# Second block: beta and decay weights as the stationary side beside the first tile, square sums and decay sums among the tiles, the last norm applied in the scan

## What is computed

```
h = rms_norm(x, norm1_w) * (1.0 + sc1) + sh1            # x: the first block's output, after its own last norm
proj = h @ w_in                                         # 1024 x (1536 + 1536 + 512 + 4 + 4 + 2048)
qa, ka, va, qkv_b, z_b, b_b, a_b, gate_a, gate_b = split(proj)
y_a = moba_attention(qa, ka, va, rel_bias)
qkv_b = silu(causal_depthwise_conv(qkv_b, conv_w))      # 4 taps, 3 * 512 channels
beta = sigmoid(b_b)                                     # 4 heads
g = -exp(a_log) * softplus(a_b + dt_bias)
o_b = gated_delta_rule(q_b, k_b, v_b, beta, g)          # q, k divided by their root of summed squares;
                                                        # cumulative sums of g per chunk of 64; scan over 4 chunks
m = sigmoid(gate_a) * (y_a @ w_up_a) + sigmoid(gate_b) * (rms_norm(o_b) * silu(z_b) @ w_up_b)
x = x + g1 * (m @ w_out)                                # then the mixture of 32 experts
```

## Time and profile before

| | us |
|---|---|
| median of 3 runs (lowest, highest) | 1450.25 (1447.91, 1450.72) |
| the profiled execution | 1449.64 |
| its span, first to last instruction | 1447.9 |
| TensorE busy | 1381.7 (95%) |
| VectorE busy | 767.1 (53%) |
| ScalarE busy | 611.1 (42%) |
| mean granted TensorE clock | 0.973 |

### The profile page before, as it was taken

How to read it: one execution, slowest core, us unless ns; L and a number is a source line. 1 busy time by engine, 2 the same in 40 slices (tenths; PEclk the granted TensorE clock), 3 DMA queues, 4 the chain that set the end, 5 groups by cost and what they waited for, 6 DMA issues and landing times.

```text
span 1447.9 us, 25571 instructions
## 1 busy us (share of the span) xinstructions
PE 1381.7 (95%) x9884; PEld 1189.3 (82%) x9884; DVE 767.1 (53%) x1338; ACT 611.1 (42%) x1016; POOL 10.6 (1%) x23
## 2 busy tenths in 40 slices
PE   6999999999999999989999999999999789999995
PEld 5899989899999798678999989889999755555543
DVE  6456646655554776346666556758546542222213
ACT  4544554533333564345444444656534321121122
POOL 0000020000000000000000000000000000000000
PEclk9999999999999899999999998999999889999999
DMA  9654345655555544367555563332134559999970
GB/s 361 127 180 146 132 161 175 242 173 173 174 174 178 215 143 132 126 239 245 190 181 186 188 235 130 131 114 76 59 102 146 199 205 409 408 405 405 406 306 29
DMA packets 80293, 289.78 MB, mean 200 GB/s; under 512 B 9536, under 2 KB 10560, under 8 KB 80064
## 3 DMA queue, kind: packets, MB, share of 16 engines
q1 hardware_dynamic: 78480, 284.65, 55.1%
q0 software_dynamic: 1712, 3.68, 1.7%
HBM read 285.14 MB, written 3.15 MB: 199 GB/s over the span
## 4 chain that ended last, share of the span: by engine, by line
PE 85%; DVE 8%; ACT 3%; issue 2%; DMA 1%; SPq 0%; DVEq 0%; ACTq 0%
PE bank L746 18%; PE bank L750 17%; PE bank L749 17%; PE bank L1364 12%; PE bank L901 2%; ACT w_hi L1440 1%; DVE ring_low L1872 1%; PE bank L1349 1%; PE bank L1325 1%; PE bank L1326 1%; PE bank L781 1%; PE bank L1350 1%; DMA ring<-weights 1%; PE bank L823 1%; DVE rstd L1904 1%
## 5 line engine op out<-in xcount | busy, mean ns | idle before, releaser
L1872 DVE TENSOR_TENSOR ring_low<-ring,w_hi 128x1024 fp32r<-128x1024 f32 x292 | 356.3, 1224 | 290.2 <-ACT w_hi L1440 287.8
L746 PE MATMUL bank<-hn_hi,w_hi 128*128 128x272 f32 (+1 forms) x1456 | 425.1, 292 | 6.1 <-DVE hn_low L1891 3.9
L750 PE MATMUL bank<-hn_hi,ring_low 128*128 128x272 f32 (+1 forms) x1456 | 418.1, 287 | 0.0
L749 PE MATMUL bank<-hn_low,w_hi 128*128 128x272 f32 (+1 forms) x1456 | 417.6, 287 | 0.0
L1440 ACT ACTIVATE w_hi<-ring 128x1024 fp32r<-128x1024 f32 x292 | 307.1, 1054 | 207.5 <-PE bank L746 174.4
L746 PEld LDWEIGHTS bank<-hn_hi,w_hi 128*128 128x128 f32 x1456 | 277.3, 190 | 12.8 <-DVE hn_low L1891 6.4
L750 PEld LDWEIGHTS bank<-hn_hi,ring_low 128*128 128x128 f32 x1456 | 277.9, 191 | 0.0
L749 PEld LDWEIGHTS bank<-hn_low,w_hi 128*128 128x128 f32 x1456 | 277.5, 191 | 0.2
L746 PE MATMUL bank<-arena_r,w_hi 128*128 128x256 f32 (+1 forms) x848 | 246.7, 291 | 9.1 <-DVE arena_r L2392 3.6
L750 PE MATMUL bank<-arena_r,ring_low 128*128 128x256 f32 (+1 forms) x848 | 243.6, 287 | 0.0
L749 PE MATMUL bank<-arena_r,w_hi 128*128 128x272 f32 (+1 forms) x784 | 225.3, 287 | 0.0
(11 more groups left out here) (386 smaller groups left out, 1620.8 us busy)
## 6 DMA issues: line engine op xcount, KB each, us to landing
ring<-weights SPq DMA_DIRECT2D x436, 512.0 KB, 4.3
tab<-weights SPq DMA_DIRECT2D x32, 512.0 KB, 6.7
w_late<-weights SPq DMA_DIRECT2D x32, 512.0 KB, 8.1
arena<-weights SPq DMA_DIRECT2D x32, 512.0 KB, 5.9
tab<-tables SPq DMA_DIRECT2D x1, 2857.0 KB, 17.6
skew<-arena POOLq DMA_DIRECT2D x1, 2048.0 KB, 46.5
h<-tokens SPq DMA_DIRECT2D x2, 544.0 KB, 4.1
tab<-skew POOLq DMA_DIRECT2D x8, 128.0 KB, 3.5
```

The source lines that it names most:

```text
L746: begun = mm(dst[:, 0:cols], wh, high(k), start=k == 0, stop=False)
L749: mm(dst[:, 0:cols], wh, low(k), start=False, stop=False)
L750: last = mm(dst[:, 0:cols], wl, high(k), start=False, stop=k == K - 1)
L1872: tt_(ring_lo[:, slot, :], ring[:, slot, :], w_hi[:, n % SPLITS, :], ALU.subtract).then_inc(S("w_lo_ready"), 1)
```

## The change

The eight weight columns of beta and decay become the stationary side: in tile 0 each k-step has, beside its own three matmuls, three with `wba` as weights (8 columns) and the 256 tokens moving, into 8 rows of `bank[4]` (`with_decay_inputs`). VectorE copies the 8 rows to `ba_rows`, and behind tile 2 two small products turn them to tokens on partitions. ScalarE reads out tiles 0 to 2 before it makes beta and softplus, VectorE makes the first tap of those tiles before it stores the inputs. The four decay sums are issued behind tile 6, and VectorE stores them before `conv(4)`. The 16 sums of squares are issued one per k-step in qka tiles 6 and 7. The first block's last norm on `h` moves to the scan: its reciprocal ahead of it, two of its 8 products in each chunk.

```
+            def with_decay_inputs(high, low, cols, ready):
...
+                dst, rows = bank[t % BANKS], bank[4][0:8, 0:cols]
...
+                pe.wait_ge(S("wba_split"), 1)
+                for k in range(DT):
+                    ready(k)
+                    cut, ba = slice(k * P, (k + 1) * P), slice(8 * k, 8 * k + 8)
+                    wh, wl = w_hi[:, n % SPLITS, cut], ring_lo[:, unit % SLOTS, cut]
+                    begun = mm(dst[:, 0:cols], wh, high(k), start=k == 0, stop=False)
...
+                    mm(rows, wba_hi[:, ba], high(k), start=k == 0, stop=False)
+                    mm(rows, wba_lo[:, ba], high(k), start=False, stop=False)
+                    last_ba = mm(rows, wba_hi[:, ba], low(k), start=False, stop=k == DT - 1)
+                    mm(dst[:, 0:cols], wh, low(k), start=False, stop=False)
+                    last = mm(dst[:, 0:cols], wl, high(k), start=False, stop=k == DT - 1)
+                last_ba.then_inc(S("ba_done"), 1)
+                last.then_inc(tile_done, 1)
...
-            dense(DT, hb, hb_lo, SEQ, split_ready("n1"))
-            pe.wait_ge(S("wba_split"), 1)
-            for tt in range(2):
-                for k in range(DT):
-                    dst, cut = bank[4][:, 8 * tt:8 * tt + 8], slice(tt * P, (tt + 1) * P)
-                    mm(dst, hn_hi[:, k, cut], wba_hi[:, 8 * k:8 * k + 8], start=k == 0, stop=False)
-                    mm(dst, hn_lo[:, k, cut], wba_hi[:, 8 * k:8 * k + 8], start=False, stop=False)
-                    last = mm(dst, hn_hi[:, k, cut], wba_lo[:, 8 * k:8 * k + 8], start=False, stop=k == DT - 1)
-            last.then_inc(S("ba_done"), 1)
+            with_decay_inputs(hb, hb_lo, SEQ, split_ready("n1"))
             for t in range(1, 12):
                 dense(DT, hb, hb_lo, SEQ)
...
-            for t in range(8):
+            for t in range(6):
                 dense(DT, hb, hb_lo, SEQ)
...
+            for t in range(2):
+                dense(DT, hb, hb_lo, SEQ, lambda k: l2_sum(DT * t + k))
             wide(DT, hb, hb_lo, [(0, P), (P, SEQ)])
...
+            for t in range(3):
+                raw_tile(t)
+            highs(at["qkvb"] + 3)
+            act.wait_ge(S("ba_split"), 2)
             fn(M("beta", 0, 8), M("b", 0, 8), ACT.Sigmoid).then_inc(S("beta_ready"), 1)
...
             lows(at["qkvb"])
             dve.wait_ge(S("ba_done"), 1)
+            nc.vector.tensor_copy(ba_rows, bank[4][0:8, 0:SEQ]).then_inc(S("ba_split"), 1)
+            for t in range(3):
+                conv_first(t)
+            lows(at["qkvb"] + 3)
+            dve.wait_ge(S("ba_done"), 2)
...
+            norm_scale("final", SEQ)
             dve.wait_ge(S("u_stored"), 1)
...
+                for k in range(2 * c, 2 * c + 2):
+                    stt(h[:, k, XC], h[:, k, XC], V("final", k), rstd[:, 0:SEQ], ALU.mult, ALU.mult).then_inc(normed, 1)
```

More of the change, by code:

```diff
@@ L1050, in _ @@
             assert pos[1] == at["qkvb"]
-            dense(DT, hb, hb_lo, SEQ, split_ready("n1"))
-            pe.wait_ge(S("wba_split"), 1)
-            for tt in range(2):
-                for k in range(DT):
-                    dst, cut = bank[4][:, 8 * tt:8 * tt + 8], slice(tt * P, (tt + 1) * P)
-                    mm(dst, hn_hi[:, k, cut], wba_hi[:, 8 * k:8 * k + 8], start=k == 0, stop=False)
-                    mm(dst, hn_lo[:, k, cut], wba_hi[:, 8 * k:8 * k + 8], start=False, stop=False)
-                    last = mm(dst, hn_hi[:, k, cut], wba_lo[:, 8 * k:8 * k + 8], start=False, stop=k == DT - 1)
-            last.then_inc(S("ba_done"), 1)
+            with_decay_inputs(hb, hb_lo, SEQ, split_ready("n1"))
             for t in range(1, 12):
                 dense(DT, hb, hb_lo, SEQ)
[L1064 to L1068, removed]
+                if t == 2:
+                    pe.wait_ge(S("ba_split"), 1)
+                    for tt in range(2):
+                        last = mm(bank[4][:, 8 * tt:8 * tt + 8], ba_rows[:, tt * P:(tt + 1) * P], ident[0:8, 0:8],
+                                  start=True, stop=True)
+                    last.then_inc(S("ba_done"), 1)
+                if t == 6:
+                    pe.wait_ge(S("g_ready"), 1)
+                    g = M("g", 0, 8)
+                    for j, name in enumerate(("upto", "chunk", "half0", "half1")):
+                        last = mm(bank[5][:, 8 * j:8 * j + 8], C(name), g, start=True, stop=True)
+                    last.then_inc(S("g_summed"), 1)
             pe.wait_ge(S("g_stored"), 1)
@@ L1084, in _, with l2_sum @@
             pe.wait_ge(S("beta_rows"), 1)
-            for p in range(2 * NP):
+            def l2_sum(p):
                 last = mm(bank[4][:, p:p + 1], l2sq[:, p * P:(p + 1) * P], ones[:, 0:1], start=True, stop=True)
-            last.then_inc(S("l2_summed"), 1)
+                if p == 2 * NP - 1:
+                    last.then_inc(S("l2_summed"), 1)
+            for t in range(2):
+                dense(DT, hb, hb_lo, SEQ, lambda k: l2_sum(DT * t + k))
             wide(DT, hb, hb_lo, [(0, P), (P, SEQ)])
@@ L1660, in _, with raw_tile @@
             fn(rms[:, 0:SEQ], bank[6][:, 0:SEQ], ACT.Sqrt, bias=eps_col(RMS_EPS), scale=1.0 / D).then_inc(rooted, 1)
-            highs(at["qkvb"])
-            act.wait_ge(S("ba_split"), 1)
+            tile[0] = at["qkvb"]
+            def raw_tile(t):
+                src, free = take()
+                fn(raw_b[:, t, CONV - 1:], src[:, 0:SEQ], ACT.Copy).then_inc(free, 1)
+            for t in range(3):
+                raw_tile(t)
+            highs(at["qkvb"] + 3)
+            act.wait_ge(S("ba_split"), 2)
             fn(M("beta", 0, 8), M("b", 0, 8), ACT.Sigmoid).then_inc(S("beta_ready"), 1)
@@ L1668, in _ @@
             fn(M("sp", 0, 8), M("sp", 0, 8), ACT.Ln, bias=eps_t[:, 2:3]).then_inc(S("softplus_ln"), 1)
-            tile[0] = at["qkvb"]
             def conv_silu(first):
@@ L1674, in conv_silu @@
                     fn(cb[:, t, :], cb[:, t, :], ACT.Silu).then_inc(S("conv_silu"), 1)
-            for t in range(12):
-                src, free = take()
-                fn(raw_b[:, t, CONV - 1:], src[:, 0:SEQ], ACT.Copy).then_inc(free, 1)
+            for t in range(3, 12):
+                raw_tile(t)
             conv_silu(0)
@@ L2170, in conv @@
                     for t in range(t0, t0 + 4):
-                        if j == 0:
-                            lows(at["qkvb"] + t)
-                            wait_stored(dve, at["qkvb"] + t)
                         x, w = raw_b[:, t, j:j + SEQ], V("conv", t * CONV + j)
                         if j == 0:
-                            last = ts_(cb[:, t, :], x, w, None, ALU.mult)
+                            if t > 2:
+                                last = conv_first(t)
                         else:
@@ L2192, in _ @@
             nc.vector.tensor_copy(M("H", 0, 16), bank[5][:, 16:32]).then_inc(S("g_stored"), 1)
+            conv(4, at["qkvb"] + 7)
+            lows(at["qkvb"] + 11)
             dve.wait_ge(S("g_exp"), 1)
```

20 lines of the change are left out of this document (15 added, 5 removed).

## The result

The changed kernel took 1435.89 us (median of 4 runs, 1431.91 to 1437.53), beside 1449.08 us (1445.77 to 1450.72) for the kernel before on the same chip: a ratio of 0.9909, 95% interval 0.9888 to 0.9931. The prediction said 1435.7. The profiled execution is the fastest of the four.

What follows compares the result with a forecast made beforehand. TensorE, holding 85% of the chain of waits, was taken as the bound, losing time to slow work and waits. Terms -16.7 + 4.4 - 1.57 gave -13.9, so 1449.64 became 1435.7 us; range 1430.5 to 1441.5.

Steps and rivals of the forecast that it cites:

- Tile 0: qkvb tile 0: VectorE's splits cover the added beta and decay matmuls except the last step's three, +0.36 us.
- Block, clock, turning products, rows: Up to qka tile 0: block, clock, idle time and broadcast rows save, added products cost; start 16.7 us earlier.
- ScalarE's small chain and tile 7: ScalarE's 3.35 us chain moves between its tiles 2 and 3; qkvb tile 7's weights stay covered by 3 us.
- The new waits: TensorE at qka tiles 4 and 5 waits 2.5 and 1.9 us for weights through ScalarE and VectorE, +4.4 us.
- Square sums and va: Sums among qka tiles 6 and 7 cost the same 3.48 us; va at full clock takes 11.2, -1.57 us.
- The norm in the scan: Reciprocal ahead of VectorE's copy, products before waits for TensorE: cost nothing, cover 1.2 us.
- no new wait: At qka tiles 4 and 5 ScalarE's chain overlaps better and no idle time comes: 1431.3 us, 15%.
- The fall of the clock at tile 0: Clock still falls in qkvb tile 0, 1.5 us lost; one half of a 19% rival, 1438.7 with both.
- The fall behind the new idle time: Clock falls after the new qka idle time, 1.5 us lost; other half of a 19% rival, 1438.7 with both.
- Larger waits: ScalarE late at qkvb tile 7, or the copy late in the scan: 1440 to 1446 us, 7%.
- a slow first tile: qkvb tile 0: the three added matmuls don't fit the 0.80 us steps, 2.5 us more, 1438.2, 4%.
- vanishing square sums: qka tiles 6 and 7: the sums' 32 passes hide behind dense matmuls, 3.5 us more won, 1432.2, 5%.

Runs made afterwards that it cites:

- experiment 5: Changed kernel with the beta and decay products of k-steps 1 to 7 of tile 0 left out (21 of 24 matmuls): 1434.19 us, ratio 0.9923.
- the second profile: The unedited changed kernel measured and profiled once more, on one chip with the kernel whose ScalarE chain was reordered: 1436.34 us, ratio 0.9924.
- Experiment 4: Changed kernel with ScalarE's SiLUs and squares behind its first qka tile and VectorE's decay differences moved up: 1432.67 us, ratio 0.9904.
- experiment 7: The changed kernel with ScalarE's SiLUs and squares moved later and VectorE's differences earlier, run once more beside the changed kernel: 1431.64 us, ratio 0.9891.
- experiment 2: Changed kernel with the 16 square sums back in one block behind qka tile 7: 1436.09 us, ratio 0.9935.
- experiment 3: Changed kernel with the first block's last norm back between conv(0) and the store of the decay sums: 1442.99 us, ratio 0.9978.
- experiment 1: Changed kernel with the decay sums back behind qkvb tile 11 and their store back behind conv(4): 1435.15 us, ratio 0.9922.
- experiment 6: Changed kernel with ScalarE's SiLUs and squares later, VectorE's differences earlier, decay sums back behind tile 11 and their store behind conv(4): 1435.03 us, ratio 0.9937.
- experiment 10: Kernel before the change with only ScalarE's SiLUs and squares moved later and VectorE's decay differences moved up: 1450.64 us, ratio 1.0012.
- experiment 9: Kernel before with only the beta and decay inputs changed; decay sums, their store, square sums and norm as before: 1441.87 us, ratio 0.9956.

## Why the prediction was right, step by step

The forecast hit in its total and in nearly all of its terms; each of them by the marks above. That the total is off by only 0.2 us is in part luck: the prediction counted from 1449.64, the median before came out at 1449.08, and the interval of the ratio spans 6 us (a gain of 10.0 to 16.2). The gain in the stretch, 13.76 against 13.9, and its parts are the better test.

*Tile 0.* From its first matmul to tile 1's: 867.01 - 860.83 = 6.18 us, and 869.61 - 863.80 = 5.81 in the kernel before: 0.37 more, +0.36 predicted. A matmul with 8 stationary columns thus cost no more than the splits cover, and experiment 5 gives 0.41 for all but the first three.

*Block, clock, turning products, rows.* From tile 0's first matmul to the first of qka: 903.35 - 860.83 = 42.52, before 923.13 - 863.80 = 59.33. That is 16.81 us less, 16.7 predicted. Tile 3 follows the turning products after 0.54 (0.45 predicted), and from it to the decay rows there are nine tiles and the decay sums in 26.56 us, 9 x 2.84 + 0.95 = 26.51 by the rows of before. The term that varies is the clock in tile 0 and 1: full in the changed kernel's first profile, fallen in the second, where it took 1.1 us of these back.

*ScalarE's small chain and tile 7.* It took 879.84 - 876.49 = 3.35 us, as before. VectorE finished tile 7's weights at 881.26 + 1.23 = 882.49 and TensorE began the tile at 885.58, so the cover was 3.1 us, with 3 predicted. The prediction miscounted here: it set three table loads against the 3.35 us, and the chain holds two. ScalarE's timeline, with the third load ahead of the chain, while it waits for VectorE:

```profile
874.87 1.28 ACT L1701 ACT_TABLE_LOAD   x1
...
876.72 1.28 ACT L1702 ACT_TABLE_LOAD   x1
...
878.34 1.28 ACT L1705 ACT_TABLE_LOAD   x1
```

Each takes the 1.28 us that the Trainium skill gives for a load (ScalarE: Activation LUTs, What ACT_TABLE_LOAD costs). With the page's drain of 1.38 us the two switches alone would be 5.3 us, by an estimate from its figures; the whole chain took 3.35, so the trace disagrees on the drain. The sum went by the 3.35 us, so the miscount did not touch it.

*The new waits.* +4.4 predicted from a chain of 17.3 us and a second one of 4.7. The first wait was 2.43 (2.5), and from one wait to the next passed 4.77 (4.7). From qka tile 0 to va the changed kernel needs 934.28 - 903.35 = 30.93 and the one before 949.40 - 923.13 = 26.27: +4.66. Experiment 4 takes away 4.32, and experiment 7 5.38 against the second profile, 1.1 of it the clock in tile 0. I had named the mechanism right but not all of its forms: the second wait shows as idle time or as a slow tile, by the clock after the first. So the line "idle rows of 2.5 and 1.9 us" was wrong for the first profile (2.43 and 0.17) and right for the second (2.42 and 1.72), while the sum held in both. The idle rows of experiments 2, 3 and 5 are as in the first (2.39 to 2.43, then 0.16 to 0.21).

*Square sums and va.* No gain and no loss in themselves (0.222 us each against 0.218), and va in 945.40 - 934.28 = 11.12 us, 11.2 predicted, 1.65 less than before. Experiment 2 gives 1.54 for both.

*The norm in the scan.* VectorE's copy at 1039.13 ends 1.16 us before TensorE's row at 1040.71 (both in the timelines above), with no idle time in front of it: a cover of 1.2, as predicted. From the rows behind va to the span's end the four kernels with the norm early take 485.7 to 487.6 us, 486.5 on average, and the eight with the norm in the scan 484.7 to 488.9, 486.3 on average. It costs nothing that these runs can tell.

*The rivals.* Without the new waits the time would be experiment 4's, which is what "no new wait" (1431.3) said, but the chain did not overlap by itself. The fall of the clock at tile 0 is real in one execution of ten, at 1.1 us where I took 1.5. The fall behind the new idle time, the other half of that rival, came in the first profile (0.53 and 0.62 above) and cost nothing where I took 1.5, since the weights of tile 5 came no sooner. Larger waits, a slow first tile, vanishing square sums and a clock that stays low over tiles 1 to 11 (it was back at 1.00 at 870 us even in the profile in which it had fallen) are refuted by rows shown above.

*The signs.* Tile 1 was to start within 0.5 us of 870.0. It started at 867.01, since this execution reached the mark 3.0 us earlier; counted from the mark, the start would be at 870.02 in the profile before, so the sign should have been tied to a mark. A clock of 0.50 in tiles 0 to 3 was to make the prediction wrong. It showed in the second profile, and that kernel's median was still 1436.34: this sign was too strict for a loss of 1.1 us.

What the prediction had not seen is how the parts hang together. It summed the store's 3.48 and its clock's 2.36 as a gain of their own and the new waits as a loss of their own. Experiments 1 and 6 show them as one thing: the move of the store is worth nothing as long as ScalarE's chain holds back the weights of qka tiles 4 and 5, and 2.1 us when it doesn't. And one condition, the norm out of VectorE's way, stood in the prediction as a place of "cost nothing" and as the reason for the idle 3.48 us; experiment 3 shows that it is worth 4.45, all of it at qkvb tile 10, where the prediction did not look. The best version that these runs have is experiment 4's: 0.9891 of the kernel before (0.9875 to 0.9907).

What stays open: why the clock falls in tile 0 in one execution of the same kernel and not in another, and why it fell behind some idle times and not behind others (last section).

## What to carry to other kernels

When a bottleneck engine is brought forward, sum up each helper's chain from the last thing that it took from that engine to the next thing that it owes: here 17.5 us from the end of tile 11 through ScalarE and VectorE, against 15.0 of TensorE's own work, gave the new wait to within 0.1 us (2.5 against 2.43). Then look at what in that chain is not owed (here 16 activations with no early reader) and put it behind: moving it cost nothing that the whole-kernel ratios can tell (experiment 10), and it was worth 4.3 us only once the change had made that chain the last. In this kernel a block of small products costs twice, once by itself and once in the clock of what follows (square sums: 3.48 us and 1.65); spread among dense ones it costs once.

## What the runs showed of the hardware

The same idle time does not always cost the clock. In experiments 1 and 6 TensorE does the same ahead of the decay rows: dense tiles at 1.00, the decay sums, and 2.10 us of idleness. Behind it the two stood so, experiment 1 first:

```profile
904.00:906.00 2.00, 2.00 (x11) 2.00 (x11) 0.00 (x0) 2.00 (x8) 0.00 (x0) 0.50 0.00 0
```

```profile
902.00:904.00 2.00, 2.00 (x18) 2.00 (x19) 0.17 (x1) 0.12 (x2) 0.00 (x0) 1.00 0.00 0
```

Ahead of qkvb tile 10, 2.78 us of idleness were followed by 0.51 in experiment 3, and a longer 3.33 us by 1.00 in experiment 9 (rows above). The rows don't name the reason; it is left open. So a term for the clock behind an idle time is a chance, not a sum: ahead of the decay rows 1.7 us or nothing.

TensorE was busy for 1.49 of 2.00 us in tile 0 of experiment 5 and kept 1.00, while the changed kernel's second profile, with more products in the same tile, fell to 0.50. Fewer products at this place did not bring the clock down, and more did not hold it up.

Three products with 8 stationary columns fit into a step of 0.80 us together with three of 128: all 24 of them made tile 0 0.37 us longer, 6.18 beside 5.81. And a product with one moving column, in float32, costs 0.218 us in a block and 0.222 among dense ones (experiment 2).
